# Weights split in place: four raw-and-low buffers and three high ones instead of three, two and two

## What is computed

```python
def swiglu(xn, w_in, w_out):
    gu = xn @ w_in
    return (jax.nn.silu(gu[..., :D_FF]) * gu[..., D_FF:]) @ w_out
...
for i in range(DEPTH):
    h = h + mixer_i(rms_norm(h, g_i))          # attention, then mLSTM
    h = h + swiglu(rms_norm(h, ffn_norm[i]), ffn_w_in[i], ffn_w_out[i])
```

## Time and profile before

| | |
|---|---|
| median of three runs | 2985.64 us |
| lowest, highest | 2983.21, 2987.95 us |
| profiled execution, first to last instruction (span) | 2983.2 us |
| PE, DVE, ACT, POOL busy | 97%, 67%, 40%, 12% |
| mean granted TensorE clock | 0.992 |
| read from DRAM over the span | 438.6 MB, 147 GB/s |

### The profile page before, as it was taken

The page is one execution under the profiler, slowest core; times in us unless marked ns, Lnnn a source line. Parts: engine busy times, 40 slices in busy tenths (PEclk is TensorE's granted clock), DMA queues, the critical chain, the costliest instruction groups (busy, mean ns, idle before and its releaser), DMA issues.

```text
span 2983.2 us, 43523 instructions
## 1 busy us (share of the span) xinstructions
PE 2888.3 (97%) x18080; PEld 2524.0 (85%) x18080; DVE 2004.9 (67%) x3284; ACT 1202.5 (40%) x1993; POOL 349.9 (12%) x542
## 2 busy tenths in 40 slices
PE   7999999989999999999999999999999999998998
PEld 7999998889997778888866888888888888877898
DVE  7776887668655557777745677777777777554665
ACT  5444544554444444223314533223243222443543
POOL 0000001000022220000131100011010000243000
PEclk9999999999999999999999999999999999999999
DMA  7544675347655424555473255553535555465453
GB/s 241 168 159 152 216 229 190 120 161 234 204 125 81 72 64 147 157 167 169 132 190 107 80 168 163 169 165 124 170 120 164 168 163 169 117 96 86 142 184 128
DMA packets 362277, 451.85 MB, mean 151 GB/s; under 512 B 12656, under 2 KB 332432, under 8 KB 362080
## 3 DMA queue, kind: packets, MB, share of 16 engines
q1 hardware_dynamic: 326976, 329.83, 34.1%
q0 software_dynamic: 34944, 118.65, 16.9%
q10 hardware_dynamic: 160, 0.59, 0.1%
HBM read 438.60 MB, written 1.05 MB: 147 GB/s over the span
## 4 chain that ended last, share of the span: by engine, by line
PE 79%; DVE 12%; ACT 5%; DMA 2%; issue 1%; POOL 1%; DVEq 0%; SPq 0%; ACTq 0%
PE ps L1352 23%; PE ps L1354 23%; PE ps L1353 23%; DVE lo L1932 4%; PE ps L1530 1%; ACT hi L1602 1%; PE ps L1373 1%; PE ps L1517 1%; DVE NB L1963 1%; DMA NB<-in_na_rpb 1%; PE ps L1375 1%; PE ps L1374 1%; DVE MX L2008 1%; PE ps L1505 1%; DVE XN L1969 1%
## 5 line engine op out<-in xcount | busy, mean ns | idle before, releaser
L1352 PE MATMUL ps<-XN,hi 128*128 128x256 f32 (+1 forms) x3184 | 1048.8, 329 | 32.9 <-DVE XN L1949 9.9
L1353 PE MATMUL ps<-XN,hi 128*128 128x256 f32 (+1 forms) x3184 | 1029.9, 323 | 0.0
L1354 PE MATMUL ps<-XN,lo 128*128 128x256 f32 (+1 forms) x3184 | 1029.6, 323 | 0.0
L1932 DVE TENSOR_TENSOR lo<-raw,hi 128x1024 fp32r<-128x1024 f32 (+1 forms) x626 | 739.2, 1221 | 250.6 <-ACT hi L1602 245.4
L1602 ACT ACTIVATE hi<-raw 128x1024 fp32r<-128x1024 f32 (+1 forms) x626 | 620.6, 1040 | 443.5 <-PE ps L1354 440.7
L1352 PEld LDWEIGHTS ps<-XN,hi 128*128 128x128 f32 x3184 | 610.6, 192 | 106.6 <-issue 17.4
L1354 PEld LDWEIGHTS ps<-XN,lo 128*128 128x128 f32 x3184 | 610.8, 192 | 46.1
L1353 PEld LDWEIGHTS ps<-XN,hi 128*128 128x128 f32 x3184 | 611.2, 192 | 44.8
L2008 DVE CUSTOM_DVE_ANT_0 MX<-MW,C 128x1024 bf16<-128x1024 f32 x384 | 477.2, 1243 | 130.7 <-DMA MW<-in_mod_w 123.8
L1352 PE MATMUL ps<-H,hi 128*128 128x512 f32 (+1 forms) x1072 | 380.2, 355 | 0.0
L1353 PE MATMUL ps<-H,hi 128*128 128x512 f32 (+1 forms) x1072 | 379.7, 354 | 0.0
(11 more groups left out here) (255 smaller groups left out, 3194.8 us busy)
## 6 DMA issues: line engine op xcount, KB each, us to landing
raw<-in_mlp_w SPq DMA_DIRECT2D x128, 1024.0 KB, 5.3
MW<-in_mod_w POOLq DMA_DIRECT2D x192, 512.0 KB, 3.8
raw<-in_ffn_w_in SPq DMA_DIRECT2D x44, 1024.0 KB, 5.4
raw<-in_attn_w_in SPq DMA_DIRECT2D x36, 1024.0 KB, 4.9
raw<-in_na_wqkv SPq DMA_DIRECT2D x24, 1024.0 KB, 5.0
raw<-in_ffn_w_out SPq DMA_DIRECT2D x16, 1024.0 KB, 5.1
raw<-in_mlstm_w_in SPq DMA_DIRECT2D x12, 1024.0 KB, 5.1
raw<-in_cv_w SPq DMA_DIRECT2D x12, 1024.0 KB, 6.2
```

Source lines behind the costliest of these rows:

```text
L1352: e.matmul(out, whi, xhi, start=first, stop=False)
L1353: e.matmul(out, whi, xlo, start=False, stop=False)
L1354: i = e.matmul(out, wlo, xhi, start=False, stop=last)
L1932: e.tensor_tensor(lo[:, a:b], raw[:, a:b], hi[:, a:b].bitcast(F32), ALU.subtract).then_inc(*low.says(("lo", j, i), ("spent", j) if i else ...
```

## The change

The low half of a unit is written over its raw weights: `raw` and `lo` are the same four memory blocks of 8 KB a partition, and there are three `hi` buffers. Together 56 KB a partition, as before. A unit can be split one unit earlier, so three units ahead of the one in work at the most. The load of unit j+4 now waits until PE has used unit j. DVE's split names one wait less (ACT's piece, for which it waits, already waited for it).

```diff
-RAW = 3
-HL = 2
+RAW = 4
+HL = 3
 NBANK = 6
@@ allocate
-    m.raw = [sb(f"raw{i}", [P, 2048]) for i in range(RAW)]
+    with ExitStack() as st:
+        m.raw = [sb(f"raw{i}", [P, 2048], F32, st) for i in range(RAW)]
+    m.lo = [sb(f"lo{i}", [P, 2048], F32R) for i in range(RAW)]
     m.hi = [sb(f"hi{i}", [P, 2048], F32R) for i in range(HL)]
-    m.lo = [sb(f"lo{i}", [P, 2048], F32R) for i in range(HL)]
@@ Plan.take
                 i = self.unit_next
-                if i > j and (i - j > HL or (i >= RAW and i - RAW not in self.known_raw)):
+                if i - j > HL:
                     break
@@ slot_of
-    h = p.slot.get(j, 0)
-    return tuple(a[h][:, 0:kt * cols].rearrange("p (k n) -> p k n", k=kt) for a in (m.hi, m.lo))
+    halves = m.hi[p.slot.get(j, 0)], m.lo[j % RAW]
+    return tuple(a[:, 0:kt * cols].rearrange("p (k n) -> p k n", k=kt) for a in halves)
@@ sync: load
         if j >= RAW:
-            w.wait_ge(("spent", j - RAW))
+            w.wait_ge(("used", j - RAW))
@@ vector: split
-        raw, hi, lo = m.raw[j % RAW], m.hi[p.slot[j]], m.lo[p.slot[j]]
+        raw, lo, hi = m.raw[j % RAW], m.lo[j % RAW], m.hi[p.slot[j]]
         cuts = cuts_of(p, j)
-        before = p.split_before[j]
-        w.wait_ge(("raw", j), None if before is None else ("used", before))
+        w.wait_ge(("raw", j))
         for i in only or (0, 1):
             a, b = cuts[i:i + 2]
             w.wait_ge(("hi", j, i))
             e.tensor_tensor(lo[:, a:b], raw[:, a:b], hi[:, a:b].bitcast(F32), ALU.subtract).then_inc(
-                *low.says(("lo", j, i), ("spent", j) if i else None))
+                *low.says(("lo", j, i)))
```

More of the change, by code:

```diff
@@ L262, in __init__ @@
         self.pace, self.credit, self.parts = 0.0, 0.0, 0
-        self.made, self.known_raw = set(), set()
+        self.made = set()
         self.norms, self.rs_user, self.sa_user, self.sq_user = 0, None, None, [None, None]
@@ L288, in split @@
             self.do("split", j)
-            self.known_raw.add(j)
         self.late.append(split)
@@ L489, in first_norm @@
         self.do("split", 1)
-        self.known_raw.update((0, 1))
         self.sa_user = ("first_ones", KT - 1)
```

## The result

| | before | change |
|---|---|---|
| median | 2985.40 us (7 runs) | 2990.64 us (7 runs) |
| lowest, highest | 2983.21, 2987.95 | 2986.87, 2999.27 |
| ratio | | 1.0027, 95% interval 1.0017 to 1.0036 |
| mean granted clock | 0.992 | 0.986 in the profiled run, 0.988 to 0.989 in the others |

The change made the kernel 5 us slower; 11 us faster (2974.5 us) were forecast, with 2967 to 2984 us as the range. Medians in this document leave out two executions of 4742.37 us (experiment 11) and 7299.86 us (before), over 1.5 times as long as all others of their kernels.

The account below looks back on a forecast made before the run. PE, busy 97% of the 2983.2 us span, was taken to bound the kernel, so only its waits and the clock could be won. 12.0 - 2.0 + 1.1 = 11.1 us, from 2985.6 to 2974.5 us; range 2967 to 2984 us.

Parts of the forecast that it names:

- All 12.0 us go.: PE's waits for lo in all stages: splitting one unit earlier removes them, 9.3 + 1.5 + 1.2 us.
- DVE in place: DVE's split, lo overwriting raw: no slower or faster than before, 0 us on the path.
- Just hidden: Start: C lands later, unit 4's split is ready at 42.7, needed at 42.9; 1.3 us lost if C is 1.5 later still.
- I treat it as spread: Second rival, bias tables' DMAs: loads at PE's pace shift table times, 2979 or 2969 us; chance 0.05 to the slower side.
- it already waits: Bias tables: four by 5 us would be 20, but only about 5 us reach PE either way.
- Clock: Low-clock stretch behind the 1.85 us wait: gone with the wait, gain 1.1 us, bounds 0 and 2.2.
- The 1.85 us at 2770 lie behind the tables, just ahead of the norm, and count: Last neighbourhood stage: this PE wait for lo, removed, reaches the end in full.
- 1.45 us and 0.5 us: Last neighbourhood stage's start and mLSTM with L1373: removed waits not reaching the end, 2.0 us taken off.
- what queues behind it on ACT is as late as before: ACT's half of the split: it waits for PE as before, its 440.7 us in 73 waits stay.
- nothing lands late: Raw loads in 512-column stages: ACT asks 10.9 us after issue, against landings of 5.3 median, 13.1 at worst overall.
- the third rival: Late loads, slower: ACT and DVE stand at splits until raw lands, 34 us over 68 feed-forward units, 3008 us; chance 0.07.
- first one (stages take it back): Short convolution and start: PE runs into other waits, gain only 5.0 us, 2980.6 us; chance 0.21.

Follow-up runs that it names:

- experiment 11: The kernel of 4 with each bias table from a stage's third on cut to one transfer of four; 2977.36 us.
- 4: C early: the change with the positions and the two C loads issued ahead of load 4; 2986.59 us, ratio 1.0009.
- 9: The kernel of 4 with ten loads of the neighbourhood stages waiting until the bias table they had run into has landed; 2980.98 us, ratio 0.9989.
- 14: The kernel of 9 with the splits of units 129, 281 to 283, 141 to 143 and 185 to 187 one unit later; 2970.67 us, ratio 0.9947.
- 10: The kernel before with each bias table from a stage's third on cut to one transfer of four; 2984.59 us.
- 13: The kernel of 9 with the splits of units 129, 281, 282 and 283 one unit later; 2973.63 us, ratio 0.9965.
- 15: The change with nothing but the ten splits of 14 one unit later; 2980.69 us, ratio 0.9990.
- experiment 16: The kernel of 14 with the split of unit 81 in the mLSTM stage one unit later too; 2974.59 us.
- second profile: The change with an added load gate that never applied, so the change again; 2992.12 us in 12 runs, the profiled run 2990.89 us.
- 1: The change with two high buffers instead of three; 2992.78 us, ratio 1.0022.
- 2: The kernel before with its loads also held back until PE is done with the unit three ahead; 3000.05 us, ratio 1.0052.
- 8: The kernel of 4 with the modulation rows cut to 64 of 1024 columns; 2985.09 us.
- 12: The kernel of 9 with the modulation rows cut to 64 of 1024 columns; 2979.43 us.

## Why the prediction was wrong

The gain came nearly as summed. Four costs had been put at 0 or at a spread of either sign: C's later load, the bias tables, the norm behind unit 280 and one late raw load. By the experiments they cost 4.1 to 5.5 us (4), 5.6 us (9) and, the last two with the stage ends like them, 6.6 us (14 less 9, without the 3.7 us gained at unit 185). That is 16 to 18 us, and 16.1 lie between the forecast and the result.

**Right but for 0.6 us: the lead.** "All 12.0 us go." Waits for lo fell from 10.8 us to 0.6, the one at 38 us went, and the seven groups of the table that hold only gains (0-3, 21-40, 63-74, 174-184, 221-229, 237-269, 279-280) come to -13.4 us. With the losses of start, tables and stage ends out, the kernel is 13.7 us under before. Of these, 3.7 us are the gain at unit 185, which isn't the lead's; the other 10.0 are near the 11.1 that I summed, and how near is partly luck, as small losses stay in that no term had. DVE in place cost nothing: lo took 1219 ns, before 1221.

**Wrong, "Just hidden", the start (4 to 5 us).** ACT started on C at 36.24 us where I had 33.7 at the latest: SP issued the first of its two loads at 26.89, near the 26.5 worked out, but the second at 27.36, and that took 8.9 us to land, not the 7.2 of the earlier trace rows. So unit 4's split came late and PE waited 0.57 us for it; this is the case "if C lands 1.5 us later still". What failed more was the question. I asked whether PE's next split would be in time, not where DVE's backlog would come out. It came out at 76.60 us, where before PE had no wait, and at 101.47, where before it had one of 0.39 us, with a low clock behind it (timeline of PE, then the stretch 102 to 106 us, columns as in the earlier trace rows):

```profile
76.60 2.23 PE L1407 MATMUL ps<-QK 128*128 128x256 f32 x12 [1.02 <-DVE QK L2066]
...
101.47 0.87 PE L1415 MATMUL ps<-cst,PB 128*128 128x128 f32 x6 [2.10 <-DVE PT L2092]
```

```profile
102.00:106.00 4.00, 4.00 (x25) 4.00 (x23) 2.15 (x3) 0.87 (x2) 0.00 (x0) 0.60 0.00 0
```

From unit 3 to unit 20 PE was idle for 3.3 us more and busy for 1.9 us more. Experiment 4 shows that C and the positions are the cause.

**Wrong, "I treat it as spread", the tables (6 to 8 us).** I had the mechanism, a price of a hit and the loads' move, and then let "it already waits" cap it at 5 us of either sign. The price was read too simply: the 9.71 and 4.60 us of the earlier trace rows are pieces of the chain, not times of tables, and that view has further pieces of 5.20, 8.24 and 5.23 us, so "others 4.60" isn't so. Of the stage's 16 tables, not four, each took 6.7 to 11.6 us. PE's wait for PB rose by 3.8 us in this stage (17.5, I had 1 to 2), and units 270 to 278 lost 8 to 11 us. The rest is the clock. From the start of unit 269 to that of unit 278, before and with the change (columns as in the earlier trace rows):

```profile
2611.01:2735.01 124.00, 118.10 (x776) 94.25 (x774) 60.56 (x126) 51.03 (x102) 51.64 (x69) 1.00 0.61 94
```

```profile
2615.97:2748.87 132.90, 122.37 (x777) 97.98 (x775) 58.46 (x125) 50.96 (x102) 47.31 (x74) 0.96 0.62 92
```

PE is idle for 4.6 us more and busy for 4.3 us more, with the clock at its lower level for 10.2 us of it, before for none. My "Clock" term could only win something; that a longer wait also costs at the lower clock, nearly its own length again here, had no term. The old loads weren't clear of the tables either: 16 of 32 had one near. But ten of the loads lay 0.5 to 1.8 us ahead of the table, and these tables took 7.9 us in the mean; the six with a load 2.3 to 3.2 us behind their start took 10.3. With the change all ten lie behind it. Experiments 9 to 11 show the tables' part.

**Wrong, "The 1.85 us at 2770 lie behind the tables, just ahead of the norm, and count" (4 us).** PE won the 1.85 us and the clock's 1.1 in units 279 and 280 (3.2 us measured) and lost them at the norm behind, because its residuals stand in DVE's list behind splits. The wait moved from lo to SA and grew. Experiments 13 to 15 show it. I had taken off 1.45 us and 0.5 us for exactly this reason at the two other places, and not looked at DVE's order here. In the mLSTM I took off 0.5; units 75 to 127 lost 0 to 1.4. A step of 1.3 or 2.8 us stands at unit 79 in every kernel with three high buffers, 1.3 of it PE's wait for WT, a buffer of the mLSTM cells (1.6 us, before 0.3). The one try at it, experiment 16, left it as it was, and its cause stays open.

**Wrong in one place, "what queues behind it on ACT is as late as before".** I set the loads' lateness against PSUM banks. Six loads were newly late where I had counted seven, but by 13.5 us together where I had 6, and the one of 8.64 us stood ahead of an evacuation for which PE had a use at once. Units 125 and 126 are worked on together, so the splits of 128 and 129 stand in a row on ACT, and ACT asked for unit 129 2.1 us after its issue, where I had 6.0 at the least and, for such a stage, "nothing lands late". The landing itself took 10.7 us behind a bias table (10.8 in the second profile), so 3 of the 8.64 us would have come with a landing in the median's 5.2 us too. The rule of the Trainium skill (DMA: Bandwidth & Descriptors, Rules for kernel authors: issue early, wait late) pointed at this; the 8.64 us agree with it, though the 34 us of the third rival did not come.

**Clock.** I expected one low stretch fewer. At its place it went: unit 279 took 7.50 us before and 5.92 with the change, 1.6 us less where I had 1.1. But a stretch of 6.8 us stands behind the new wait at unit 281, before 3.4, and others stand behind other new waits. The sum of the low stretches rose from 50 us to 87 in the change's first profile and 69 in its second, and was 49 in the thirteenth. PE's idle time alone doesn't set it: experiments 1 and 2 had as much as the change (100.6 and 105.4 us) with 57 us low.

**The rivals.** The first one (stages take it back) names the right place in the short convolution and the start, but I let it only give back what was gained there. The collisions of the modulation rows are real (DVE's wait for MW 123.8 to 187.5 us) and cost PE a wait for YH of 4.5 us at unit 230 in the change's first profile, and a like step in five of the eleven profiles with three high buffers and whole modulation rows, the change's first among them; with the rows cut it was absent in both. The medians with the rows cut are 1.5 us lower (4 against 8, 9 against 12), no more than the spread, so it is no part of the main cause. Why it appears in some runs only stays open.

## What to carry to other kernels

A condition that is moved from one engine's signal to another's moves a transfer in time, and what it costs is read from what else is in the queues at that moment: here the bias tables, C and the positions, far more than the loads' own deadlines. A wait that PE gains or loses is priced with the clock behind it: in the last neighbourhood stage 4.6 us more of waiting made 8.9 us. Work that is taken off PE's waits ahead of a norm or another chain is worth something only if the engines that run that chain are free then; look at what stands in their lists between the last product and the chain's first step. Once a buffer scheme gives room, use the lead where the compute engine streams, and leave it off at the ends of stages: ten splits moved back were worth 10 us here, and an eleventh cost 4.2 us in its stage.

## What the runs showed of the hardware

A bias table (four strided transfers) landed in 7.0 us alone and in 10.9 us with a 1 MB load issued 0.5 to 4.0 us behind its start (22 and 10 tables of the change), so a load that nobody waited for held up a transfer that the path needed by 3.9 us. With the load issued 1.5 to 1.8 us ahead of the table it took 7.1 us (six tables of before), with the load 0.5 us ahead 9.1 (four). The load suffers too: the one behind the first table took 10.7 us, where the median of all is 5.2.

PE pays for a wait twice where the clock falls behind it. With the change units 269 to 278 had 4.6 us more idle time and, with 10.2 us at a granted clock of 0.5 (1.2 GHz) instead of none, 4.3 us more busy time; units 229 to 236 in the first profile 3.8 and 1.7 us, with 6.8 us at 0.5.

And the changed kernels scatter more: in one session 26 runs of before lay within 7.8 us, twelve of the change within 13.4, eleven of C early within 17.0 (2979.69 at a mean clock of 0.992, 2996.70 at 0.985).
